# Latents' attention: probabilities divided in place by ScalarE and turned by plain transposes, in place of products with diagonal matrices

## The reference, cut to what matters

```python
s = jnp.concatenate([s_win.reshape(s_win.shape[:5] + (n_win,)), s_ctx], axis=-1)
p = jax.nn.softmax(s, axis=-1).astype(v.dtype)
...
o = (jnp.einsum('bhrjqik,brijkhd->brjqhd', p_win, v_band) +
     jnp.einsum('bhrjqc,bchd->brjqhd', p_ctx, v_ctx))
```

## Time and profile before

| | |
|---|---|
| median of 3 runs | 1949.89 us (1946.81 to 1951.14) |
| profiled execution, its own time: the span from the first to the last instruction | 1975.1 us |
| PE busy | 1811.1 us (92%) |
| DVE busy | 1291.4 us (65%) |
| ACT busy | 283.3 us (14%) |
| POOL busy | 908.3 us (46%) |
| mean granted TensorE clock | 0.971 |

### The profile page before, as it was taken

One profiled execution on the slowest core, in us unless ns is written; L12 is line 12 of the kernel. 1 busy time (PEld: TensorE's weight loads), 2 busy tenths in 40 slices (PEclk: granted clock), 3 DMA queues, 4 the chain that ended last, 5 costly groups with the idle time before them and its releaser, 6 DMA issues.

```text
span 1975.1 us, 21712 instructions
## 1 busy us (share of the span) xinstructions
PE 1811.1 (92%) x8148; PEld 1170.2 (59%) x8148; DVE 1291.4 (65%) x2583; ACT 283.3 (14%) x660; POOL 908.3 (46%) x837
## 2 busy tenths in 40 slices
PE   4888899967999899999999999998799899995997
PEld 2676744446544349997888888886544334442443
DVE  2110487879688778999988966549956533349752
ACT  0120010037300001111110100016620000000000
POOL 1010226668555412235454566657856664545500
PEclk8998999989999999999999999999999999997999
DMA  8894949898999967469999999997999999999983
GB/s 355 355 365 189 356 178 407 290 369 274 337 398 336 346 241 286 140 217 376 346 374 379 370 409 409 409 372 267 336 354 409 410 407 409 409 409 410 409 326 135
DMA packets 166713, 670.23 MB, mean 339 GB/s; under 512 B 19370, under 2 KB 19498, under 8 KB 160972
## 3 DMA queue, kind: packets, MB, share of 16 engines
q0 software_dynamic: 112512, 410.79, 55.1%
q1 hardware_dynamic: 49344, 242.24, 31.3%
q10 hardware_dynamic: 4752, 15.81, 2.1%
HBM read 659.27 MB, written 7.39 MB: 338 GB/s over the span
## 4 chain that ended last, share of the span: by engine, by line
PE 65%; DMA 13%; DVE 8%; POOL 7%; issue 4%; another core or an unknown queue 2%; ACT 1%; ACTq 0%; SPq 0%; DVEq 0%; POOLq 0%
PE psum L853 22%; PE psum L921 16%; PE psum L1014 7%; DMA arena<-in_expert_u_dram,arena 7%; POOL arena L542 7%; PE psum L979 4%; PE psum L944 3%; PE psum L947 3%; DVE arena L1425 3%; PE psum L881 2%; DMA arena<-in_w_ada_dram 2%; PE psum L956 1%; PE psum L954 1%; PE psum L698 1%
## 5 line engine op out<-in xcount | busy, mean ns | idle before, releaser
L542 POOL DMA_INDIRECT arena<-in_expert_u_dram,arena x384 | 487.2, 1269 | 349.7 <-DVE arena L1425 219.5
L1425 DVE CUSTOM_DVE_ANT_0 arena<-arena 128x1024 f32<-128x1024 f32 x384 | 460.5, 1221 | 182.4 <-DMA arena<-in_expert_u_dram,arena 172.1
L542 POOL DMA_INDIRECT arena<-in_expert_v_dram,arena x384 | 382.3, 996 | 375.5 <-DVE psum L1659 208.6
L921 PE MATMUL psum<-arena 128*128 128x512 f32 x1024 | 451.4, 602 | 24.9 <-issue 16.9
L853 PE MATMUL psum<-arena 128*128 128x256 f32 x2048 | 445.9, 381 | 4.9 <-DMA arena<-in_expert_uT_dram 4.9
L1659 DVE SCALAR_TENSOR_TENSOR psum<-arena,psum 128x1024 f32<-128x1024 f32 x254 | 327.0, 1287 | 162.1 <-DMA arena<-in_expert_v_dram,arena 132.0
L853 PEld LDWEIGHTS psum<-arena 128*128 128x128 f32 x2048 | 390.7, 191 | 58.8 <-issue 5.2
L921 PEld LDWEIGHTS psum<-arena 128*128 128x128 f32 x1024 | 196.2, 193 | 281.1 <-issue 272.0
L1014 PE MATMUL psum<-arena 128*128 128x128 f32 x1280 | 149.8, 278 | 3.6 <-issue 3.1
L1014 PEld LDWEIGHTS psum<-arena 128*128 128x128 f32 x1280 | 147.3, 195 | 5.4 <-issue 4.7
L710 PE MATMUL psum<-arena 128*128 128x512 f32 x320 | 137.7, 592 | 0.0
(11 more groups left out here) (174 smaller groups left out, 1352.1 us busy)
## 6 DMA issues: line engine op xcount, KB each, us to landing
arena<-in_expert_uT_dram SPq DMA_DIRECT2D x128, 512.0 KB
arena<-in_expert_v_dram SPq DMA_DIRECT2D x128, 512.0 KB
arena<-in_w_in_dram SPq DMA_DIRECT2D x16, 2048.0 KB
arena<-in_w_ada_dram SPq DMA_DIRECT2D x12, 2048.0 KB
arena<-in_w_query_dram SPq DMA_DIRECT2D x8, 2048.0 KB, 22.9
arena<-in_w_in_dram SPq DMA_DIRECT2D x16, 512.0 KB, 8.7
arena<-in_w_o_dram SPq DMA_DIRECT2D x4, 2048.0 KB
arena<-in_expert_u_dram,arena POOLq DMA_INDIRECT x384
```

The costliest lines, as they stand in the source:

```text
L542: pool.indirect_dma_start(slot, None, table[0], bass.IndirectOffsetOnAxis(ap=number, axis=0)).then_inc(land, 16)
L921: mm = pe.matmul(bank(2 + 2 * d + hf), own, RINGS[value_load_of(n) % RING][:, hf * HALF:(hf + 1) * HALF], start=n == 0, stop=n == NKEYS - 1)
L1425: dve.tensor_tensor_reduce(UR[b], UR[b], U2B[e], 1.0, 0.0, ALU.mult, ALU.add, DOTS[e % 2][:, k:k + 1]).then_inc(u_free, 1)
```

## The change

The diagonal buffers go. ACT multiplies the unit's 512 exponentials by the reciprocal of their sum in the score buffer itself, 128x512 in place of the 128x128 diagonal. PE turns all units with `pe.transpose` against the identity. The semaphore `diag_done` is renamed `prob_done`. ACT's wait for `pt_done`, which kept a diagonal buffer from being overwritten, goes with the buffers.

```diff
-        DIAG = [at(9728 + P * i, P) for i in range(3)]
...
                 else:
-                    pe.wait_ge(diag_done, n - 1)
+                    pe.wait_ge(prob_done, n - 1)
...
                 for i in range(4):
                     out, src = bank(2 + n % 2)[:, i * P:(i + 1) * P], s_buf(n)[:, i * P:(i + 1) * P]
-                    if n < 2:
-                        mm = pe.transpose(out, src, IDN)
-                    else:
-                        mm = pe.matmul(out, src, DIAG[n % 3], start=True, stop=True)
+                    mm = pe.transpose(out, src, IDN)
                 mm.then_inc(pt_done, 1)
...
                     if lo < n <= hi and n > 2:
-                        diagonal(n - 1)
+                        normalise(n - 1)
...
-            def diagonal(n):
+            def normalise(n):
                 act.wait_ge(recip_done, n + 1)
-                if n >= 5:
-                    act.wait_ge(pt_done, n - 2)
-                act.activation(DIAG[n % 3], IDN, ACT.Copy, scale=RINV[:, n % 3, 0:1]).then_inc(diag_done, 1)
+                act.activation(s_buf(n), s_buf(n), ACT.Copy, scale=RINV[:, n % 3, 0:1]).then_inc(prob_done, 1)
```

More of the change, by code:

```diff
@@ L302, in backbone @@
             sem("sc_done"), sem("s_scaled"), sem("win_step"), sem("max_done"), sem("exp_done"))
-        bias_masked, diag_done = sem("bias_masked"), sem("diag_done")
+        bias_masked, prob_done = sem("bias_masked"), sem("prob_done")
         recip_done, norm_done, pt_done, pt_out, pv_done, po_out = (
```

## The result

The changed kernel takes 1967.22 us (median of 4 runs, 1962.53 to 1969.87) against 1950.52 us: ratio 1.008, 95% interval 1.0061 to 1.0099, slower by some 16.7 us. Once more, beside the experiments, the ratio was 1.0069 (1.0046 to 1.0092). The forecast was 1952 us. It gave slower the greater chance than faster (0.34 against 0.09), though no clear change was its likeliest outcome (0.57). The loss of its sum was too small by a factor of six to eight: 2 us forecast, 12 to 17 measured. The range held the time only because rival 1 stretched it to 1974 us; the likeliest case spanned 1948 to 1958.

A forecast was written before the change was run, and what follows sets the result against it. DVE was taken to bound the latents' attention, though PE leads the whole kernel. Clock falls +2.4, start 0 and stage end -0.34 summed to +2.1 us on 1949.9, giving 1952 us; range 1947 to 1974.

The forecast's parts named there:

- rival 1: Latents' attention: transposes do not keep PE's clock up, it stays low for most of the stage; 1974 us, chance 0.20.
- the likeliest case: Latents' attention: PE's clock falls now and then, making DVE late at times; 1948 to 1958 us, chance 0.53.
- DVE bounds the stage at 5.66 us a pair: Steady latents' attention: DVE is full at 63.25 of 64.00 us, so pairs without a clock fall keep 5.66 us.
- The sign that DVE stays over 96% busy: Between 440 and 504 us of the profile, DVE was to remain over 96% busy if the forecast held.
- ScalarE's instruction 0.72 us: ACT's new 128x512 division in SBUF takes 0.72 us, +0.32 us a unit over the removed 0.40 us diagonal instruction.
- Its cover of 0.6 us: Exponentials are ready about 0.6 us before DVE's reciprocal starts, twice the 0.32 us that ACT's longer instruction asks.
- The turn 0.66 us shorter; PE's wait grows from 1.27 to 2.6 us: PE's turn by four transposes takes 0.43 instead of 1.09 us; its wait in each pair grows to 2.6 us.
- The clock falls, because such a wait is longer than the one before the fall in the earlier trace: Steady attention: PE's 2.6 us wait exceeds the 1.96 us before the earlier trace's clock fall, so falls are expected.
- One fall in two pairs, 0.3 us each, +2.4 us: Steady attention: 8 clock falls at 0.3 us of DVE time each, +2.4 us, bounds 0 and +11.
- 0.97 us: Steady attention: scores ready for ACT 0.34 us earlier raise the cover before DVE takes them from 0.63 us to this.
- The stage's end, -0.34 us: Last path from DVE's final reciprocal to section(1): row +0.32, turn -0.66, so section(1) starts 0.34 us earlier.
- Carried on one for one: From section(1) at 513.47 us PE works without a gap, so a shift there reaches the end in full.

The follow-up runs named there:

- e2: Changed kernel with 12 extra transposes of the identity, unread, between the two turns of each pair: 1978.74 us, ratio 0.9982 to the kernel before.
- e3: Changed kernel with 5 extra products of the identity, unread, between the two turns of each pair: 1977.29 us, ratio 0.9982 to the kernel before.
- e4: Changed kernel with PE's mix moved between the two turns of each pair: 1952.03 us, ratio 1.0001 to the kernel before.
- e6: Changed kernel with 6 extra transposes of the identity, unread, between the two turns of each pair: 1951.69 us, ratio 1.0000 to the kernel before.
- e7: Kernel before with two DVE filler dot products a pair instead of three, the others moved behind the stage: 1993.11 us, ratio 1.0075.
- e1: Changed kernel with ScalarE's 512-column division kept but PE turning by products instead of transposes: 1983.39 us, ratio 1.0012 to the kernel before.
- e8: Changed kernel with two DVE filler dot products a pair instead of three, the others moved behind the stage: 1998.86 us, ratio 1.0104 to the kernel before.
- e5: Changed kernel with ScalarE dividing only the first 128 of the 512 probabilities, transposes kept: 1951.68 us, ratio 1.0004 to the kernel before.
- a1: Changed kernel run again unaltered, for a second profile: 1964.64 us against 1952.37 for the kernel before, ratio 1.0069.
- e0: Kernel before run again unaltered, for a second profile: 1978.25 us against 1979.84, ratio 1.0000.
- e10: Changed kernel with ScalarE dividing only the first 256 of the 512 probabilities, transposes kept: 1980.23 us, ratio 1.0013 to the kernel before.

## Why the prediction came out as it did

- *DVE bounds the stage at 5.66 us a pair*: right, and shown by e2, e3, e4 and e6, which all return to it. The sign that DVE stays over 96% busy failed: it is 87% (55.87 of 64.00 us).
- *ScalarE's instruction 0.72 us*: measured 0.73. *Its cover of 0.6 us*: wrong. It was read off the exponentials, but the loop through PE has less room: 5.66 - 5.48 = 0.18 us (e7). With 0.32 us more and products kept, the pair is 5.80 us (e1), as 5.48 + 0.32 gives. With the transposes too it is 5.17 at the upper clock (e8): the 0.34 us by which the two steps together were to shorten the path are 0.31.
- *The turn 0.66 us shorter; PE's wait grows from 1.27 to 2.6 us*: the turn was a little too short, 0.50 us up to the next instruction in e2's rows and 0.59 in after's, so 0.5 to 0.6 us go. A wait of 2.33 us is seen where pairs are at 5.66 us (in after at 489.17, and in e5 without the longer ScalarE operation); in the slower rhythm it is 1.85, since mix and scores have stretched into it.
- *The clock falls, because such a wait is longer than the one before the fall in the earlier trace rows*: the fall came, the reason was too simple. 1.85 us a pair goes with a fall in each pair, and 1.68 us (e6) with none; in e5, where one pair in three or four is cold, six turns had a wait of 2.33 us before them, and four of the six led into a cold mix; in e8 1.84 us goes with few falls at first and 1.85 us with one in each pair later. The length of the wait alone does not order these, so no limit for it can be read off, as the expectation of e6 tried.
- *One fall in two pairs, 0.3 us each, +2.4 us* is the term of the sum that was mis-sized, in number and in price. After has 6.4 to 6.8 us in 11 of the 15 distances, a1 6.7 to 6.8 in 12. The cold pair is priced rightly: 0.68 for the mix and 0.95 for the scores are +1.63 on the loop's 5.17, which gives the measured 6.80. What was wrong is the cover. I took 0.97 us, which is what one late pair finds after pairs that were in time. When each pair is late, the cover is that of the loop, 5.66 - 5.17 = 0.49 us, and a fall costs 1.63 - 0.49 = 1.14 us. Over 11 pairs (after) that is 12.5 us, over 12 (a1) 13.7; the stages differ by 11.1 and 13.7. The two need not agree to the last digit: some late pairs cost less, before and e0 have a stall of 0.7 to 0.9 us in their first pairs too, and the end of the stage adds 0.5 us.
- *Rival 1* had the mechanism and, at +21 to +24 us, too high a price: 7.5 us a pair counted a cold turn and a longer way through ScalarE (1.88 us, measured 1.62). Its ground, transposes that do not count, does not hold in e2 and e6. Yet the forecast owes its range to this rival: that 1967 us lies inside it is in part luck, since the rival's price was too high and its ground was wrong.
- *The stage's end, -0.34 us*: two cold mixes come before section(1) in after, and from the last bias addition to section(1) it takes 8.05 us instead of 7.51. With the clock held (e2) it is 7.3.
- *Carried on one for one*: not refuted, and not shown closely: 13.7 us in the stage and 12.3 in the medians for a1, 11.1 and 16.7 for after.

Left open: why the clock falls in each pair once the pair is 6.8 us, and only sometimes when it is 5.66 or less. e8 shows both in one execution with the same wait; no run changes the rhythm alone.

## What to carry to other kernels

Less work for TensorE is no gain where another engine sets the rhythm, and can be a loss: check what the idle time that it leaves does to the granted clock, and price the work behind each wait at the lower level. Measure the cover of a loop by the loop's own length against the engine that bounds it (take a little of that engine's work away and look), not by how early one operand was ready once. If the clock falls in such a loop, two things gave the loss back here: filling the wait with dummy work, which kept the clock up (e2, e3, e6), and an order in which the cold work no longer stands before what the bounding engine needs (e4), which adds no work and let the clock fall.

## What the runs showed of the hardware

- Twelve float32 transposes of 128x128 in PE's wait keep the granted clock at 1.00, as five products do (e2, e3); six do as well (e6).
- Two effects whose cost alone is not told from nothing, a longer ScalarE operation (e1, ratio 1.0012) and shorter turns (e5, 1.0004), cost 0.7 to 0.8% together, because together they close a loop in which every pair runs its mix and scores at 1.2 GHz.
- The same program took 1952.4 us in one sitting and 1976.8 in another on the same chip. In the profiles with long times PE stands idle long after 1750 us, where it needs the expert values (23.6 us in e0, 26.0 in e8), in those with short times hardly at all (1.4 us in a1 and e6). Single executions differ from their sitting: before's first profile, 1975.1 us beside runs of 1950, has 24 us of it, and e10's, its fastest at 1959.68 us beside a median of 1980, has 5.9. The cause is open.
